# A two-layer decoder step on one core: the first token slot in two transfers, modulation parts by transposes, sample sums moved ahead of a copy

## The reference, cut to what matters

```
silu_c = silu(c)                                  # 9 rows in all
mod = silu_c @ w_mod[l] + b_mod[l]                # (9, 6 * 1024)
sh1, sc1, gt1, sh2, sc2, gt2 = split(mod, 6)
h = rmsnorm(x, norm1_g) * (1 + sc1) + sh1
mix = token_mixing(h)      # projections v u ga q k vr gr gb; gated MLP; retention; output product
x = x + gt1 * mix
h = rmsnorm(x, norm2_g) * (1 + sc2) + sh2
x = x + gt2 * hier_moe(h)  # 4 groups, top 2 of the 8 experts of one group, 32 experts
y = rmsnorm(x, final_g)    # after the last layer
```

## Time and profile before

| | |
|---|---|
| Median of 3 runs | 1727.54 us (1727.22 to 1728.41) |
| Profiled execution, its own time | 1724.3 us |
| Profiled execution, span from first to last instruction | 1722.7 us |
| TensorE matmul busy | 1675.0 us, 97% |
| VectorE busy | 526.5 us, 31% |
| ScalarE busy | 258.2 us, 15% |
| GpSimd busy | 46.2 us, 3% |
| Moved by DMA | 451.69 MB, mean 262 GB/s |
| Mean granted TensorE clock | 0.99 |

### The profile page before, as it was taken

How to read it: one execution, slowest core, us unless ns; L and a number is a source line. 1 busy time by engine, 2 the same in 40 slices (tenths; PEclk the granted TensorE clock), 3 DMA queues, 4 the chain that set the end, 5 groups by cost and what they waited for, 6 DMA issues and landing times. The chain is left out here.

```text
span 1722.7 us, 20395 instructions
## 1 busy us (share of the span) xinstructions
PE 1675.0 (97%) x8346; PEld 968.2 (56%) x8346; DVE 526.5 (31%) x1265; ACT 258.2 (15%) x502; POOL 46.2 (3%) x93
## 2 busy tenths in 40 slices
PE   6999999999999899999999999999999998999997
PEld 3677764445577554444447777554547765444443
DVE  1220210124611354333442212102263126233346
ACT  3110001101210231111131100010112013211111
POOL 0000000000100000000000000000010010000000
PEclk8999999999999989999999999999999999999999
DMA  9533556467943649999983336443887432899993
GB/s 400 235 138 125 217 201 256 179 245 296 406 188 135 244 148 388 421 421 421 423 345 132 127 120 256 184 147 148 327 347 301 147 134 112 329 422 421 421 421 162
DMA packets 47021, 451.69 MB, mean 262 GB/s; under 512 B 5632, under 2 KB 5888, under 8 KB 7504
## 3 DMA queue, kind: packets, MB, share of 16 engines
q1 hardware_dynamic: 43200, 409.65, 59.6%
q10 hardware_dynamic: 3456, 37.75, 5.2%
q0 software_dynamic: 272, 2.97, 0.4%
HBM read 411.16 MB, written 39.19 MB: 261 GB/s over the span
## 5 line engine op out<-in xcount | busy, mean ns | idle before, releaser
L657 PE MATMUL ps<-ring,work 128*64 128x512 f32 x1536 | 337.9, 595 | 2.9 <-ACT work L1055 2.6
L657 PE MATMUL ps<-ring,hT 128*32 128x128 f32 (+1 forms) x1920 | 319.9, 383 | 2.1 <-DMA ring<-stream 2.0
L657 PE MATMUL ps<-hT,ring 128*128 128x288 f32 x1280 | 314.4, 407 | 1.9 <-DVE work L1608 1.9
L657 PEld LDWEIGHTS ps<-hT,ring 128*128 128x128 f32 x1280 | 242.2, 190 | 71.6 <-issue 6.1
L657 PE MATMUL ps<-work,ring 128*128 128x288 f32 x1024 | 249.6, 406 | 4.1 <-issue 2.3
L657 PEld LDWEIGHTS ps<-ring,hT 128*32 128x32 f32 (+1 forms) x1920 | 154.8, 137 | 168.1 <-issue 163.0
L1055 ACT ACTIVATE work<-ps 128x512 f32<-128x512 f32 (+5 forms) x244 | 109.5, 467 | 837.4 <-PE ps L657 836.5
L657 PEld LDWEIGHTS ps<-ring,work 128*64 128x64 f32 x1536 | 111.7, 137 | 211.3 <-issue 211.0
L657 PEld LDWEIGHTS ps<-work,ring 128*128 128x128 f32 x1024 | 194.2, 190 | 58.7 <-issue 5.4
L657 PE MATMUL ps<-work 128*128 128x288 f32 (+6 forms) x800 | 189.5, 399 | 6.3 <-DVE hT L1751 2.6
L657 PEld LDWEIGHTS ps<-work 128*128 128x128 f32 (+2 forms) x800 | 125.1, 187 | 69.4 <-issue 36.4
(11 more groups left out here) (177 smaller groups left out, 846.8 us busy)
## 6 DMA issues: line engine op xcount, KB each, us to landing
ring<-stream SPq DMA_DIRECT2D x96, 2048.0 KB, 8.6
ring<-stream SPq DMA_DIRECT2D x192, 1024.0 KB, 10.2
state_sample_out<-ring ACTq DMA_DIRECT2D x16, 2048.0 KB, 10.0
state_out<-prm ACTq DMA_DIRECT2D x8, 512.0 KB, 11.4
prm<-params SPq DMA_DIRECT2D x1, 2608.5 KB, 25.8
prm<-params POOLq DMA_DIRECT2D x1, 2608.5 KB, 15.8
cst<-consts SPq DMA_DIRECT2D x1, 1649.0 KB, 19.2
xT<-x_in SPq DMA_DIRECT2D x1, 1152.0 KB, 5.4
```

Source lines behind the costliest of these rows:

```text
L657: return nc.tensor.matmul(out, lhsT, rhs, start=start, stop=stop, **k)
```

## The change

There are three parts. (1) Slot ("v", 0) of layer 0, the load with number RING, comes in two transfers, and TensorE waits for the second at k = 4 of the first product. (2) Each mod step's four parts are turned by four transposes of 128 x 128 into a bank tile of its own, and VectorE adds the four parts with a reduce and then adds the bias, for each mod step by itself: `take_mod` at the next mod step or at the fold step. The tiles "modt" take their turn in banks 0 to 6, those of fold "next" and fold "gate" stay in bank 7, and those of layer 1's mod steps 4 and 5 stand in banks 3 and 4. (3) The multiplication of the samples' sums by the gate and their addition to x move from behind y1's copy of the last pair to in front of it, as pair 14's sums are in.

```diff
+turn, waiting = 0, None
+def use_fold(b=None):
+    global turn, waiting
+    if waiting is not None:
+        use((*waiting, "modt"), turn % 7 if b is None else b)
+        turn += b is None
+    waiting = None
...
-        for _g in (g for g, group in GROUPS_OF_MODS.items() if _s == ("mod", group[0])):
-            use((_g, "modt"), YBANK)
         for _t in tiles_of(_s, _l):
             use((_l, _s, _t), turn % 7)
             turn += 1
+        if _s[0] == "mod" or _s[0] == "fold" and waiting is not None and FOLD_OF[waiting[1][1]][0:2] == (_l, _s[1]):
+            use_fold(YBANK if _s in (("fold", "next"), ("fold", "gate")) else None)
+        if _s[0] == "mod":
+            waiting = (_l, _s)
...
-HALVED = [key[1][0] == "pair" for key in LOADS]
+HALVED = [key[1][0] == "pair" or n == RING for n, key in enumerate(LOADS)]
...
             def token_major(l, step):
...
                         if step == ("v", 0) and tt == 0:
+                            if l == 0 and k == KT // 2:
+                                wait_rest(l, step)
                             pe.wait_ge(affine_ready, m * KT + k + 1)
...
             def fold_pending(group=None):
...
-                gl, name, n = FOLD_OF[step[1]]
-                key = ((gl, name), "modt")
-                wait_reads(pe, [(l, step, "modp")], free=key if n == 0 else None)
+                key = (l, step, "modt")
+                out = wait_free(pe, key, [(l, step, "modp")])
                 buf = modp[:, MOD_TURN[step[1]] % 2, :]
                 for c in range(4):
-                    at = (4 * n + c) * ROWS
-                    last = mm(ps[bank(key)][:, at:at + ROWS], buf[:, c * P:c * P + P], C("modfold"), True, True)
-                if n == len(GROUPS_OF_MODS[gl, name]) - 1:
-                    made(last, key)
+                    last = transposed(out[:, c * P:c * P + P], buf[:, c * P:c * P + P], C("ident"))
+                made(last, key)
...
+            def take_mod(group=None):
...
+                dst = mod_of(l)[:, 4 * i:4 * i + 4, :]
+                parts = wait_made(dve, key)[:, :].rearrange("p (c j r) -> p c r j", c=4, j=4)[:, :, 0:ROWS, :]
+                taken(dve.tensor_reduce(dst, parts, op=ALU.add, axis=AX.X), key)
+                settle()
+                dve.tensor_tensor(dst, dst, bias, ALU.add)
                 settle()
...
+                    if kind == "mod":
+                        take_mod()
+                        waiting.append((l, step))
+                    elif kind == "fold":
+                        take_mod((l, i))
...
                             taken(dve.tensor_tensor(hT[:, ft, SAMPLES], hT[:, ft, SAMPLES], out[:, SAMPLES], ALU.add), key)
+                        settle()
+                        hs, x_s = by_sequence(hT[:, :, :]), by_sequence(xT[:, :, :])
+                        dve.tensor_tensor(hs, hs, of_rows(gate), ALU.mult)
+                        settle()
+                        dve.tensor_tensor(x_s, x_s, hs, ALU.add)
```

More of the change, by code:

```diff
@@ L133, in use @@
     used[b] += 1
-turn = 0
+turn, waiting = 0, None
[5 more added lines that the diff above has]
+    waiting = None
 for _l in range(DEPTH):
@@ L158 @@
             use((_l + 1, "ss1"), 2)
-            if LAST_MODS[_l]:
-                use(((_l, "last"), "modt"), 3)
+            for _n, _s in enumerate(LAST_MODS[_l]):
+                use((_l, _s, "modt"), 3 + _n)
         for _f in range(KT):
@@ L1306, in of_rows @@
                 return ap[:, :, 1:ROWS].rearrange("p k (b o) -> p k b o", o=1).broadcast_to([P, k, NB, NT])
[L1308 to L1314, removed]
+            waiting = []
+            def take_mod(group=None):
+                if not waiting or group is not None and FOLD_OF[waiting[0][1][1]][0:2] != group:
+                    return
+                key = (*waiting.pop(), "modt")
+                l, i = key[1][1]
+                bias = (R("bmod") if l == 0 else bias_next)[:, 4 * i:4 * i + 4].rearrange("p (f o) -> p f o", o=1).broadcast_to([P, 4, ROWS])
+                dst = mod_of(l)[:, 4 * i:4 * i + 4, :]
[3 more added lines that the diff above has]
+                dve.tensor_tensor(dst, dst, bias, ALU.add)
                 settle()
@@ L1544, in _ @@
                     kind, i = step
-                    if kind == "fold":
-                        if step == ("fold", "start"):
+                    if kind == "mod":
+                        if l == 0 and step == ("mod", (0, 0)):
                             dve.wait_ge(head_loaded, 48)
-                        take_mods((l, i))
+                        take_mod()
+                        waiting.append((l, step))
+                    elif kind == "fold":
+                        take_mod((l, i))
                     elif kind == "scale":
@@ L1565, in _ @@
                             if i == 1:
-                                take_mods((l - 1, "last"))
+                                for last in LAST_MODS[l - 1]:
+                                    waiting.append((l - 1, last))
+                                    take_mod()
                     elif kind == "affine":
@@ L1764, in _ @@
                             dve.scalar_tensor_tensor(xT[:, k, 0:SEQ], hT[:, k, 0:SEQ], gate[:, k, 0:1], xT[:, k, 0:SEQ], ALU.mult, ALU.add)
[L1765 to L1769, removed]
                 settle()
```

## The result

The changed kernel takes 1711.43 us (median of 4 runs, 1707.46 to 1713.15), the kernel before beside it 1727.97 (4 runs): a ratio of 0.99, with a 95% interval of 0.9885 to 0.9915. That is 16.5 us, and the forecast was 10.1. The same kernel run again on another chip gave 1712.54 (6 runs, ratio 0.9903, 0.9886 to 0.992).

What follows compares the result with a forecast made beforehand. TensorE, busy for 1675.0 of 1722.7 us, was taken as the bound. The terms 0.8 + 3.5 + 1.9 + 0.45 + 1.05 + 2.2 + 0.2 gave 10.1 us off the 1727.54 median: 1717.4 us, range 1711.5 to 1722.0.

Steps and rivals of the forecast that it cites:

- the half taken back at the third routing fold: Layer 0's routing: fold saves 0.9 us at the low clock, earlier gather in the slow stretch takes half back, leaving 0.45.
- Rival 1: At the start and in layer 0's routing, slow pieces end earlier, 3.4 us more gained: 1714.0 us; chance 0.12.
- Rival 2: Ahead of the waits for hT and the choice, TensorE idles longer; two more slow pieces cost 3.4 us: 1720.8; chance 0.14.
- Rival 4: Between the projections, transposes don't keep the clock; twelve folds cost 20.4 us: 1738 us; chance 0.03.
- The fold's price: Each modulation fold on TensorE: four transposes take 0.44 us instead of 0.92, saving 0.48.
- the 3.5 of the sum: Layer 0's eight folds between the q, k and vr steps: six save 2.9 us, the last two 0.65.
- Layer 1's four: Four folds in layer 1, together 1.9 us saved.
- Rival 3: At the folds, transposes cost 0.92 us each, so 6.9 us leaves the sum: 1724.3 us; chance 0.05.
- The banks: Pair 0's gather: shifted tiles remove waits of 0.62 us (layer 0) and 1.69 (layer 1); pair 0 gains 1.05 and 2.2.
- The start: Layer 0's v projection: half the token slot lands earlier, so TensorE starts near 32.15, released by ScalarE; 0.8 us saved.
- the fold's chain behind the fourth product: At the start: copy, fold, VectorE's two operations and ScalarE's first tile run from 29.00 to near 32.15.
- Seam and samples: Between the layers 0 gained; at the end the first add follows the scatter by 0.79 instead of 0.99, saving 0.2 us.

Runs made afterwards that it cites:

- split: The kernel before with only the first token slot in two transfers: 1727.62 us, ratio 0.9999.
- both extra turns: The kernel before with gather tiles in the changed kernel's banks, layer 1's turns ahead of its gather (ratio 1.0002) or ahead of its kts step (0.9986).
- samples' sums: The kernel before with only the last pair's sums moved ahead of y1's copy: a single run, 1730.3 us.
- old fold everywhere: The changed kernel with every fold again four matmuls of 9 columns and one VectorE add, banks and order kept: 1721.06 us, ratio 0.9958.
- folds and banks alone: The changed kernel with the first token slot in one transfer and the samples' lines as before: 1714.01 us, ratio 0.9919.

## Why the forecast came out too small

- **The step that failed is the clock.** The sum gave it nothing but the half taken back at the third routing fold. Rival 1 had it give 3.4 us at two places, with a chance of 0.12 and "the folds' work is less" against it. It gave some 6.8: 13.6 us less at 0.50. The argument against was wrong. The folds are shorter, but the run with 128-column products and the one with doubled transposes show that this work holds the clock where four products of 9 columns, in the same number of records and the same time, don't. Rival 2, the clock takes back, did not win in the means, though the wait for hT grew by 0.4 us at the longest, as it said. But the clock does take back 1.6 us inside layer 1's pair 0, in eleven of the twelve profiles without the wait of 1.69 us there. That is a slow piece at a place where the prediction allowed none, and the sum counted the 1.69 in full.
- **Rival 4**, and with it the rule in the Trainium skill (TensorE: Matmul & The Clock Gate, Part 4, PE-mode transpose) that a transpose "doesn't count as PE-busy the same way", is not borne out here: with transposes 27.7 us at 0.50, with twice as many 22.3, with the old fold 36.7. The prediction priced this rival at the twelve folds between the projections, although it says itself that by the rule the sum stays as it is where long products stand around the fold. Those folds gained what the sum said.
- **The fold's price**: 0.48 us was forecast as its gain; the hold-up gives 0.92 - 0.50 = 0.42 and the shorter product behind it 0.08, together 0.50; the way from 105 to 308 us gives the 3.5 of the sum. Layer 1's four gave 2.0 (forecast 1.9). Rival 3 falls.
- **The banks**: both waits gone, as the count of turns had it. The rest moved by 2.8 ±0.8 us for 2.3, the median by only 1.1 of 1728.43: the slow stretch in layer 1's pair 0, which came with the gain, fits that.
- **The start**: releaser and time were right (31.93, forecast 32.15), and so was the fold's chain behind the fourth product: it took 31.93 - 28.76 = 3.17 us, forecast 32.15 - 29.00 = 3.15. The reason was not. I gave the 0.8 to the split; alone it gave nothing measurable, and without it TensorE started at 31.97. The DMA's wait of the earlier trace rows, which the term rests on, stands in one profile of four.
- **Seam and samples**: 0 and 0.2, as forecast.
- **Open**: why the clock falls in layer 1's pair 0 once the gather's wait is gone. Why the rest rose by 9.2 us with 128-column products, where 13 folds on the path at 0.99 - 0.50 give 6.4. One piece shows in its profile: at full clock TensorE comes to layer 0's gather 0.34 us before VectorE is done. The rough correction for the clock may hold more; no run settles it. How much of the 13.6 us each place contributes is not shown either, but the profiles point to three. Six have the old fold (before, split, both extra turns, samples' sums, old fold everywhere), three the new one without added products (changed, changed again, folds and banks alone). Up to 60 us the old ones have 6.8 to 13.7 us at 0.50 and the new ones 3.4 to 6.8; from the wait for the choice in layer 0 into the gather the old ones have 6.8 or 13.7 and the new ones 6.8; in the 60 us behind, four of the six have 3.4 and the new ones nothing. Three profiles are few: two of the old ones lie at the new ones' value in the routing.

## What to carry to other kernels

Where TensorE is the bound and its clock moves between two levels, count the time at the low level in every run, from the mean granted clock, and compare kernels with and without it: here an arithmetic that was right to about 1 us missed two fifths of the gain. When very short products stand near waits, weigh what replaces them by what it does to the clock as well as by its duration. And fill the remaining waits with products nobody reads, sized to end before the wait does: that was worth another 7 to 8 us, and some twice as many gave about half of it back.

## What was not expected of the hardware

- Folds of ordinary 128-column products cost 0.49 us more than the transposes at each of 13 places, 6.4 us, and made the kernel only 3.4 to 4.5 us slower than the changed one: 17.8 us at 0.50 instead of 27.7.
- The clock fell with no long wait in front: from 593.20 on it was 0.50, behind the stretch from 589.80 to 593.20 in which TensorE was busy for 1.65 of 3.40 us and waited once, for 1.75 us. At the start it stayed at 1.00 behind a stretch with a wait of the same length: busy for 1.77 of 3.50 us, waited for 1.73.
- In layer 1's pair 0 the clock is at 0.50 for a stretch behind a wait of 1.35 us in eleven of the twelve profiles in which the gather no longer waits 1.69 us some 20 us earlier, and in none of the four in which it does. The 48 records behind that wait take 12.22 us in the changed kernel's profile and 10.58 in that of before.
- VectorE's reduce of 144 elements from PSUM took 0.31 us, as long as the add of 144 from PSUM although it writes 36, and the add behind it 0.20.
